# Who makes the low halves of the first 32 expert blocks: six of them moved from GpSimd to VectorE, the rest in two pieces instead of four, and two small steps put elsewhere in the order

## The reference

```python
def peer_ffn(xn, w_query, sub_keys, expert_u, expert_v):
    q = (xt @ w_query).reshape(T, PEER_HEADS, 2, QUERY_HALF)
    s = jnp.einsum('thpd,hpnd->thpn', q, sub_keys)
    s_top, i_top = lax.top_k(s, PEER_TOPK)             # 16 of 128, for 8 heads x 2 halves
    cand = s_top[:, :, 0, :, None] + s_top[:, :, 1, None, :]
    g_s, sel = lax.top_k(cand, PEER_TOPK)              # 16 of 256, for 8 heads
    idx = jnp.take_along_axis(cand_idx, sel, axis=-1)  # which of 16384 experts
    g = jax.nn.softmax(g_s, axis=-1)
    ...
        a = jnp.einsum('td,thkd->thk', xc, u)
        w = gc * jax.nn.gelu(a, approximate=False)
        return jnp.einsum('thk,thkd->td', w, v)
```

## Time and profile before

| | |
|---|---|
| median of 3 runs | 2910.21 us |
| profiled execution | 2913.14 us, its span 2911.3 us |
| PE busy | 2801.7 us, 96% of the span |
| DVE busy | 2300.0 us, 79% |
| ACT busy | 1379.6 us, 47% |
| POOL busy | 816.1 us, 28% |
| granted TensorE clock, mean | 0.987 of full speed |

### The profile page before, as it was taken

The page is one execution under the profiler, slowest core; times in us unless marked ns, Lnnn a source line. Parts: engine busy times, 40 slices in busy tenths (PEclk is TensorE's granted clock), DMA queues, the critical chain, the costliest instruction groups (busy, mean ns, idle before and its releaser), DMA issues.

```text
span 2911.3 us, 48985 instructions
## 1 busy us (share of the span) xinstructions
PE 2801.7 (96%) x19360; PEld 2600.1 (89%) x19360; DVE 2300.0 (79%) x3460; ACT 1379.6 (47%) x1553; POOL 816.1 (28%) x663
## 2 busy tenths in 40 slices
PE   5999899999999999999999999999999999999999
PEld 3888788888889888789999989999999999999998
DVE  7788768888875765667959978888778959978887
ACT  4444545454444544454445554444444445545444
POOL 2310313113131120005992013321006981023221
PEclk9999999999999999999999999999999999999999
DMA  7777247777843465334457779999454557779997
GB/s 298 282 278 278 73 144 268 284 251 277 286 159 116 171 217 178 116 116 172 176 179 259 263 260 325 372 377 376 160 188 174 178 197 256 256 276 333 361 390 295
DMA packets 161902, 699.99 MB, mean 240 GB/s; under 512 B 15240, under 2 KB 61488, under 8 KB 105536
## 3 DMA queue, kind: packets, MB, share of 16 engines
q1 hardware_dynamic: 122720, 559.65, 53.2%
q10 hardware_dynamic: 20576, 70.85, 6.6%
q0 software_dynamic: 18432, 67.12, 6.3%
HBM read 667.07 MB, written 30.42 MB: 240 GB/s over the span
## 4 chain that ended last, share of the span: by engine, by line
PE 54%; POOL 5%; DVE 4%; DMA 2%; ACT 2%; issue 1%; ACTq 0%; SPq 0%; DVEq 0%
PE pp L1426 6%; PE mz L1426 6%; PE pp L1353 6%; PE pp L628 5%; POOL w_lo L2990 5%; PE mz L1428 3%; PE pp L1355 3%; PE pp L1428 3%; PE pp L1331 3%; PE pp L1333 3%; PE pp L1332 3%; PE pp L630 2%; PE pp L639 2%; PE pp L641 2%; PE pp L640 2%; DMA raw<-expert_v 2%
## 5 line engine op out<-in xcount | busy, mean ns | idle before, releaser
L1534 ACT ACTIVATE w_hi<-raw 128x2048 fp32r<-128x2048 f32 (+1 forms) x486 | 893.3, 1839 | 396.7 <-DMA raw<-expert_v 203.6
L2108 DVE TENSOR_TENSOR w_lo<-raw,w_hi 128x2048 fp32r<-128x2048 f32 (+1 forms) x400 | 874.1, 2186 | 240.5 <-ACT w_hi L1534 239.4
L2990 POOL TENSOR_TENSOR w_lo<-raw,w_hi 128x512 fp32r<-128x512 f32 x288 | 402.3, 1437 | 718.5 <-ACT w_hi L1534 717.6
L628 PE MATMUL pp<-hs,w_hi 128*128 128x512 f32 x1408 | 511.1, 406 | 24.2 <-POOL hs L3073 12.6
L630 PE MATMUL pp<-hs,w_lo 128*128 128x256 f32 x1408 | 398.7, 283 | 0.0
L1426 PE MATMUL mz<-w_split,w_hi 128*128 128x448 f32 x1024 | 355.0, 377 | 7.0 <-issue 7.0
L628 PEld LDWEIGHTS pp<-hs,w_hi 128*128 128x128 f32 x1408 | 269.3, 191 | 99.0 <-DVE w_lo L2108 11.5
L1426 PE MATMUL pp<-w_split,w_hi 128*128 128x448 f32 x1024 | 353.1, 376 | 2.2 <-DVE w_split L2818 1.9
L628 PE MATMUL pp<-us,w_hi 128*128 128x512 f32 x960 | 345.4, 403 | 9.0 <-DVE both L2127 4.2
L1353 PE MATMUL pp<-hs,w_hi 128*128 128x448 f32 x1024 | 328.9, 377 | 1.3 <-POOL w_lo L2990 1.3
L1331 PE MATMUL pp<-hs,w_hi 128*128 128x224 f32 x1024 | 285.0, 278 | 12.5 <-POOL w_lo L2990 12.2
(11 more groups left out here) (362 smaller groups left out, 5800.7 us busy)
## 6 DMA issues: line engine op xcount, KB each, us to landing
raw<-expert_u SPq DMA_DIRECT2D x128, 1024.0 KB, 4.9
raw<-expert_v SPq DMA_DIRECT2D x128, 1024.0 KB, 7.3
raw<-ffn_in SPq DMA_DIRECT2D x88, 1024.0 KB, 4.8
ada_raw<-ada ACTq DMA_DIRECT2D x116, 512.0 KB, 5.2
raw<-ffn_down SPq DMA_DIRECT2D x64, 704.0 KB, 5.3
raw<-out_w SPq DMA_DIRECT2D x16, 1024.0 KB, 4.7
raw<-hgrn SPq DMA_DIRECT2D x16, 1024.0 KB, 4.8
raw<-query SPq DMA_DIRECT2D x16, 1024.0 KB, 4.7
```

Of the source, the lines that this page charges most:

```text
L628: mm(outp, w_hi[:, slot, a:a + P], rhs[:, k0 + k].rearrange("p a t -> p (a t)"), start=(k0 + k == 0), stop=False, skip_group_check=True)
L1534: f(w_hi[:, slot, 0:n], raw[:, slot, 0:n], ACT.Copy).then_inc(hi_ready, 1)
L2108: v.tensor_tensor(w_lo[:, slot, 0:n], raw[:, slot, 0:n], w_hi[:, slot, 0:n].bitcast(F32), ALU.subtract)\
L2990: last = g_.tensor_tensor(w_lo[:, slot, a:a + n], raw[:, slot, a:a + n], w_hi[:, slot, a:a + n].bitcast(F32), ALU.subtract)
```

## The change

1. In the first half VectorE makes the low part of six odd chunks, those of the pairs 5, 7, 9, 12, 14 and 15 (chunks 11, 15, 19, 25, 29 and 31), at fixed places of the selection (`split_odd`). GpSimd makes the other 26, and each in two instructions of 128 x 1024. Its four in the second half are in two as well. TensorE waits for the six on `lo_shared`.
2. TensorE's transposes of the routes stand behind the first chunk of the second half and no more ahead of it; ScalarE's copy and VectorE's tables move with them.
3. At the seam between the second half and `expert_v`, ScalarE's `high(0)` stands ahead of its last copy of the second half, and VectorE's `low(0)` ahead of the last `join`.
4. VectorE's wait for all Gelus of the first half stands later, and TensorE's loop of the first half is written out.

```diff
-PIECES = 4
+PIECES = 2
+DVE_HALVES = (5, 7, 9, 12, 14, 15)
+POOL_HALVES = (2, 6, 10, 14)
...
# TensorE
-                for rp, pair, half, lap in pairs_of(pe, ph):
+                for rp, pair, half, lap in each_pair(ph):
                     for j in range(2):
                         n = 2 * rp + j
-                        pe.wait_ge(lo_ready, 2 * pair + j + 1)
+                        if j and rp in DVE_HALVES:
+                            pe.wait_ge(lo_shared, shared_count(q // 2, 0, rp))
+                        else:
+                            pe.wait_ge(lo_ready, 2 * pair + j + 1)
...
+                        if n == 0:
+                            turn_routes(l)
...
# ScalarE
-                act.wait_ge(rt_mm, l + 1)
-                f(route[:].rearrange("p a t -> p (a t)"), mz.rearrange("p a n -> p (a n)")[:, 0:3 * T], ACT.Copy).then_inc(rt_cp, 1)
...
+                        if n == 1:
+                            act.wait_ge(rt_mm, l + 1)
+                            f(route[:].rearrange("p a t -> p (a t)"), mz.rearrange("p a n -> p (a n)")[:, 0:3 * T], ACT.Copy)\
+                             .then_inc(rt_cp, 1)
...
+                        if n == HALF_CHUNKS - 1:
+                            act.wait_ge(gate_spilled[1], unit_count(l + 1, 1))
+                            act.wait_ge(g_used, STEPS * (l + 1))
+                            high(0)
...
# VectorE
+            def split_odd(l, rp):
+
+                pair = plan[("expert_u", 2 * l)].pair0 + rp
+                slot = 2 * (pair % 2) + 1
+                dve.wait_ge(hi_ready, 2 * pair + 2)
+                v.tensor_tensor(w_lo[:, slot], raw[:, slot], w_hi[:, slot].bitcast(F32), ALU.subtract).then_inc(lo_shared, 1)
...
                         top16(top_v[:, tb, hp], top_i[:, tb, hp], s_keys[:, tb, hp])
+                        if tb and hp == 10:
+                            split_odd(l, DVE_HALVES[2])
                     for h0 in (0, 4):
                         candidates(tb, h0)
+                    split_odd(l, DVE_HALVES[3 * tb])
                     look_up(tb)
                     if tb == 0:
...
+                        split_odd(l, DVE_HALVES[1])
...
+                split_odd(l, DVE_HALVES[4])
                 dve.wait_ge(best_e, l + 1)
...
+                split_odd(l, DVE_HALVES[5])
...
+                        if n == 1:
+                            take_routes()
                         if n:
                             join(n - 1)
+                        if n == LEAD + 1:
+                            dve.wait_ge(gelu_done, HALF_CHUNKS * (2 * l + 1))
...
-                join(HALF_CHUNKS - 1)
...
                 low(0)
+                join(HALF_CHUNKS - 1)
...
# GpSimd
-                        split(pair + 1, 1 - half, j, lo_ready)
+                        if not (j and rp + 1 in DVE_HALVES):
+                            split(pair + 1, 1 - half, j, lo_ready, 2 if rp + 1 in DVE_HALVES else 1)
```

More of the change, by code:

```diff
@@ L184, in opened, with shared_count @@
         yield from pairs_of(eng, ph.part(a, b - a))
-PIECES = 4
+PIECES = 2
+DVE_HALVES = (5, 7, 9, 12, 14, 15)
+POOL_HALVES = (2, 6, 10, 14)
 DOTS = 26
-def pool_half(rp):
-    return rp % 4 == 2
+def shared_count(l, second, rp):
+    before = (len(DVE_HALVES) + len(POOL_HALVES)) * l + len(DVE_HALVES) * second
+    return before + (POOL_HALVES if second else DVE_HALVES).index(rp) + 1
 def row_steps(m):
@@ L454, in build @@
         few_made, few_mm, few_cp = sem("few_made"), sem("few_mm"), sem("few_cp")
-        few_in, lo_pool = sem("few_in"), sem("lo_pool")
+        few_in, lo_shared = sem("few_in"), sem("lo_shared")
         row_in = [sem(f"row_in{i}") for i in range(ROW_RING)]
@@ L1334, in up, with turn_routes @@
                         last.then_inc(w_used, 1)
+            def turn_routes(l):
+                pe.wait_ge(rt_src, l + 1)
+                pe.wait_ge(few_cp, l + 1)
+                for r in range(3):
+                    for tb in range(TB):
+                        src = gate_n[:, tb].rearrange("p h k -> p (h k)") if r == 2 else ij_f[:, r, tb]
+                        last = nc.tensor.transpose(mz[:, r // 2, ((r % 2) * 2 + tb) * P:((r % 2) * 2 + tb + 1) * P], src, ident)
+                last.then_inc(rt_mm, 1)
             def up_joined(ph, l, spread):
@@ L1340, in up_joined @@
                         n = 2 * rp + j
-                        if j and pool_half(rp):
-                            pe.wait_ge(lo_pool, 4 * l + rp // 4 + 1)
+                        if j and rp in POOL_HALVES:
+                            pe.wait_ge(lo_shared, shared_count(l, 1, rp))
                         else:
@@ L1394, in peer @@
                 up(ph.part(8, ph.pairs - 8), 2 * l)
[L1395 to L1401, removed]
                 g0 = STEPS * l
@@ L1977, in up_kept, with high @@
                             gelu(gate_a[:, bass.ds(4 * rp + 2 * j, 2), :], pair, half, j)
+                c0 = 2 * plan[("expert_v", 2 * l)].pair0
+                def high(m):
+                    if m < HALF_CHUNKS:
+                        src = gate_a[:, 2 * m:2 * m + 2, :]
+                    else:
+                        rp, j = (m - HALF_CHUNKS) // 2, m % 2
+                        act.wait_ge(w_mul, HALF_CHUNKS * (l - 1) + m + 1)
+                        src = act_in[:, rp % RING, j].rearrange("p e u t -> p e (u t)")
+                    act.wait_ge(w_used, c0 + m - 1)
+                    f(w_split[:, m % 2, :, 0], src, ACT.Copy).then_inc(ws_hi, 1)
                 def gelu_joined(n):
@@ L2029, in peer @@
                 gelu_joined(HALF_CHUNKS - 1)
[L2030 to L2046, removed]
                 for g in range(P // EXP_J):
@@ L2744, in peer, with take_routes @@
                  .then_inc(rt_src, 1)
[L2745 to L2750, removed]
-                g0 = STEPS * l
+                split_odd(l, DVE_HALVES[5])
+                g0 = STEPS * l
+                def take_routes():
+                    dve.wait_ge(few_cp, l + 1)
+                    dve.wait_ge(rt_cp, l + 1)
+                    v.tensor_copy(route_b[:, 0:2], route[:, 0:2])
+                    link(v.tensor_scalar(route_b[:, 2], route[:, 2], GATE_SCALE, None, ALU.mult))
+                    link(v.scalar_tensor_tensor(rest[:], route[:, 2], GATE_SCALE, route_b[:, 2], ALU.mult, ALU.subtract))
+                    link(v.tensor_copy(route_b[:, 3], rest[:]))
                 def build(n, b):
@@ L2777, in peer @@
                 ph = plan[("expert_u", 2 * l + 1)]
-                dve.wait_ge(gelu_done, HALF_CHUNKS * (2 * l + 1))
                 dve.wait_ge(lo_ready, 2 * ph.pair0 + 2)
@@ L2793, in peer @@
                             build(n - LEAD + 1, (n - LEAD + 1) % 2)
-                        if not pool_half(rp + 1) or rp == ph.pairs - 1:
+                        if rp + 1 not in POOL_HALVES:
                             split_next(ph, rp, pair, half, j)
@@ L2982, in experts, with split @@
             def experts(l):
-                def split(pair, half, j, done):
+                def split(pair, half, j, done, by=1):
                     slot = 2 * half + j
@@ L2991, in split @@
                                                 ALU.subtract)
-                    last.then_inc(done, 1)
+                    last.then_inc(done, by)
                 def fetch(i):
@@ L3013, in experts @@
                 for rp, pair, half, lap in each_pair(ph):
-                    if pool_half(rp):
-                        split(pair, half, 1, lo_pool)
+                    if rp in POOL_HALVES:
+                        split(pair, half, 1, lo_shared)
                 for i in range(ROW_RING, 2 * FEW_STEPS):
```

## The result

The changed kernel takes 2923.6 us (median of 15 runs, 2911.3 to 2933.3) where the kernel before, run beside it on the same chip, takes 2914.2: a ratio of 1.0032, 95% interval [1.0019, 1.0045], or 9.4 us more. That is under the 0.5% which the prediction called no change, but with so many runs the interval is clear of nought: the forecast of a sum of 0 was wrong by some 9 us. The profiled execution took 2926.4 us, its span 2924.5 against 2911.3.

A forecast was written before the change was run, and what follows sets the result against it. TensorE, busy 96%, was held to lose only by waits, mostly on GpSimd, and its slow clock. First halves +6.8 and seam -6.8 us summed to 0, leaving the median at 2910 us, range 2893 to 2926.

The forecast's parts named there:

- Chunk 11, +1.8: First half, layer 0: TensorE waits 1.8 us for VectorE's split of chunk 11, with no fall of the clock.
- `look_up` stays 23.6: VectorE's `look_up` and `id_u`, between the splits of chunks 11 and 15, keep taking 23.6 us.
- Long look-up: Slower rival: small VectorE instructions in `look_up` wait longer for GpSimd's pieces, +22 us for two layers, 2932; chance 0.12.
- Chunk 25, idle 4.3: First half: TensorE waits 4.3 us for VectorE's split of chunk 25 and loses 1.7 to the clock.
- Chunk 29 is in time: First half: VectorE's split of chunk 29 ends before TensorE asks for it, so no wait was charged.
- The bound above (+8.1 a layer): Upper bound for a layer's first half: both long waits cost one more GpSimd half, 2 x 2.37 us, giving +8.1.
- The clock: TensorE's clock falls after long waits: 1.7 us lost after 2.29 us of idle time, none after 1.44 us.
- Chunk 19 is in time: First half: VectorE reaches chunk 19's split some 20 us after chunk 15's, TensorE not before 1452, so no wait.
- The seam, -6.8: Seam to `expert_v`: an earlier low part saves 2.8 us in layer 0 and 4.0 in layer 1, idle time and clock.
- Part 1: Fewer, longer GpSimd instructions, two per chunk at 2.37 us each; charged nothing, GpSimd's waits in TensorE expected to go.
- VectorE's wait for the exponential, down to about 6 us: VectorE's wait for ScalarE's late exponential, ahead of `gate_n` and chunk 31's split, falls from 20 to about 6 us.
- In time: Faster rival: VectorE's splits come before TensorE asks, all GpSimd waits go and the seam gains, 2881 us; chance 0.13.

The follow-up runs named there:

- e2_pieces: The kernel before with PIECES = 2 alone, all 32 low parts of the first half still at GpSimd: ratio 0.9949 to the kernel before.
- e8_no15: The changed kernel with chunk 15 given back to GpSimd, five splits at VectorE: ratio 1.0059 to the kernel before.
- e10_whole: The changed kernel without VectorE's splits, GpSimd's 32 in one piece each: 2906.6 us, ratio 0.9980 to the kernel before.
- e11_again: The changed kernel run once more, nothing altered: ratio 1.0025 to the kernel before.
- e9_four: The changed kernel, six splits at VectorE kept, with GpSimd's splits in four pieces as before: ratio 0.9982 to the kernel before.
- e4_timed: The changed kernel with three splits at VectorE (chunks 13, 19, 27) instead of six: ratio 0.9977 to the kernel before.
- the second profile: Profile of the changed kernel run once more, nothing altered: ratio 1.0025 to the kernel before.
- e1_seam: The kernel before with the change's part 3 alone (high(0) and low(0) earlier at the seam to expert_v): ratio 0.9981 to the kernel before.
- e5_none: The changed kernel without VectorE's six splits, GpSimd making all 32 in two pieces: ratio 0.9915 to the kernel before.
- e6_two: The changed kernel with two splits at VectorE (chunks 13 and 27) instead of six: 2897.7 us, ratio 0.9933 to the kernel before.

## Why the prediction was wrong, step by step

With the transposes counted where they were before, the first halves cost 15.3 us and not 6.8, and the seam gave 3.7 us and not 6.8. That is 11.6 us in the profiles, beside 9.4 between the medians.

**GpSimd's waits all go: right.** Its instructions take 2.4 us (median 2405 ns of 120, predicted 2.37).

**Chunk 11, +1.8: right** (1.80, 1.79). VectorE's split took 4.10 us, 1.8 of it a wait for GpSimd's first half of chunk 12.

**`look_up` stays 23.6: right here** (24.1). Chunk 15's wait of 4.3 us was 4.55 and 4.56. The rival "Long look-up" was right on the mechanism and on its condition: where GpSimd makes all 32, the same stretch is 30.0 us (e2_pieces), and 28 to 30 where it skips chunk 11 but not 15 (e8_no15). In the changed kernel it skips both. The Trainium skill, page "SBUF — State Buffer", section "Who interferes with whom", says that a VectorE instruction in a mode that uses two ports, as `tensor_scalar` can be, and a GpSimd one shut each other out for the whole instruction. The 4.53 us of e10_whole's `id_u`, a `tensor_scalar` that takes 0.21 us in the changed kernel, agree with it.

**Chunk 25, idle 4.3: near** in layer 1 (4.01), where the first half came out at +3.4 as predicted. In layer 0 it was 1.70, since the clock had held TensorE back 1.5 us longer and VectorE began the split 0.9 us earlier.

**"Chunk 29 is in time": the step that failed.** It had no working, and the prediction's own numbers speak against it. Measured: 4.90 us of idle time in layer 0 (4.19 in e11_again), and in time by 0.60 us in layer 1. VectorE's split of chunk 25 was put at 1489.3. From there to the end of the last `look_up` the kernel before took 22.5 us (the cast at 1474.87 in the earlier trace rows to `gate_e`), so the split of chunk 29 ends at 1489.3 + 22.5 + 2.2 = 1514.0. TensorE, by the same sums, asks at 1489.3 + 1.7 + 4 x 5.36 = 1512.4. It is 1.6 us late with no new wait for GpSimd at all. In layer 0 such waits came on top, at `eq`, `gate_e` and the split itself. VectorE's timeline:

```profile
1499.12 4.40 DVE L2717 TENSOR_TENSOR eq<-sel_b,iota_b 128x2048 bf16<-128x2048 bf16 x1
...
1507.14 2.53 DVE L2761 TENSOR_TENSOR gate_e<-best_v 128x256 f32<-128x256 f32 x1
1509.60 4.44 DVE L2133 TENSOR_TENSOR w_lo<-raw,w_hi 128x2048 fp32r<-128x2048 f32 x1
```

and GpSimd beside the last two:

```profile
1507.01 4.88 POOL L3020 TENSOR_TENSOR w_lo<-raw,w_hi 128x1024 fp32r<-128x1024 f32 x2 [5.63 <-ACT w_hi L1544]
```

GpSimd sat idle for 5.63 us and began 0.13 us before `gate_e`. From the first cast to the end of `gate_e` it took 23.9 us instead of 22.5, and the split 4.44 instead of 2.29: 3.5 us on top of the 1.6, against the 4.90 measured. In layer 1 the last steps of the selection fell into GpSimd's idle time (that stretch took 20.5 us) and chunk 29 was in time. That layer 1 came out as forecast is therefore partly luck: what the forecast left out happened not to fall there. With four pieces chunk 29 was in time in both layers, by 3.4 and 3.6 us (e9_four). The bound above (+8.1 a layer) had priced such meetings for the two long waits alone.

**The clock: mis-sized.** I took 1.7 us for every wait over 2 us. That held in layer 1 (0.5 x 3.1 = 1.6). In layer 0 it was 3.3 behind chunks 15 and 29 each. By chunk starts, layer 0 lies at +5.4 us against before from chunk 16 on (layer 1: +3.9), at +2.4 (+3.3) at chunk 28 and at +11.1 (+3.9) at chunk 31. So of the 7.3 us by which layer 0's first half exceeds the forecast, all comes at chunk 29 and its clock; the 1.5 us lost at chunk 15 were given back at chunk 25.

**"Chunk 19 is in time": right, but by the waits ahead of it.** Without them it was 8.5 us late (e4_timed).

**The seam, -6.8: too much.** With the transposes counted where they were, both second halves with the seam together gave 3.7 us, and 4.1 in the second profile. Layer 0 was as predicted or better: idle 1.51 (2.0 predicted), and no fall of the clock behind it. Layer 1 has 3.23 where it had 3.20, with the clock at 0.50 behind it. The prediction took ScalarE and VectorE to be as far at the seam as in the kernel before. Here VectorE's splits start at 2580.36 and 2585.64, 5.28 us apart, where TensorE takes 6.0 per chunk: join, Gelu, high part and split follow each other as a chain that was late and catching up. What the long idle times share is ScalarE's wait of 3.8 us or more for a spill (above). That chain is read from the traces; no run took it apart, and its cause stays open. Alone the seam is worth 5.6 us, interval 1.5 to 10 (e1_seam).

**Part 1 "charged at nothing": wrong.** Beside the six splits the two pieces cost 15 us against four (e9_four): the prediction had the longer pieces only as waits of VectorE at chunks 11, 15 and 25, and not on the way to chunk 29. And since nothing was worked out for the pieces without the splits, it could not see that alone they were worth 15 us, and that the splits turn this round.

**VectorE's wait for the exponential, down to about 6 us**: 11.1 and 8.5. The exponential follows Gelus of a TensorE that is itself late, by 11 us in layer 0 and 4 in layer 1.

The rival "In time" (2881) has its number nearly reached by a kernel without any split at VectorE (e5_none, 2892), but not its mechanism: with two splits that were in time (e6_two) the first halves were no shorter than with none.

## What to carry to other kernels

Work given to a second engine at fixed places of its own stream must be checked place by place, each with both clocks written out, the last one too: most of the error of this forecast's first half sits in a place that was not written out. A wait that is removed makes TensorE earlier at every place behind it, so the places behind must be checked again (chunk 19). Where two engines shut each other out, the length of an instruction on one is what a short instruction on the other may have to wait; shorten GpSimd's pieces if VectorE is the urgent one, lengthen them if GpSimd is, and do not move work across in the same step without trying each alone. The simple half of a compound change may be the whole gain: here `PIECES = 2` and the seam without the splits take 25 us off.

## What the runs showed of the hardware that was not expected

- A VectorE instruction that waits for GpSimd does not always get the next turn: one of 1.4 us took 28.4 while GpSimd ran 29 pieces back to back (e1_seam).
- After waits of the same length (4.55 and 4.56 us) the granted clock stayed at 0.50 for 6.6 us in one layer and 3.1 in the other. After waits of 1.80 and 1.70 us it stayed at 1.00 in one case and fell for 3.2 us in the other:

```profile
1486.50:1489.70 3.20, 3.20 (x17) 3.20 (x17) 3.20 (x2) 0.05 (x1) 3.20 (x2) 0.50 0.63 264
```

- GpSimd's 128 x 1024 piece takes 2.35 to 4.45 us, median 2.41 (the changed kernel), and the 128 x 2048 one 4.51 to 6.66, median 4.62 (e10_whole).
